# The expert stage of a diffusion step: plain fp32 on four column blocks, 96 tokens in three groups, in place of three rounded products of 128

## The chip, the cores and the metric

One core of a Trainium2 chip. The metric is the device time of one execution in microseconds. Lower is better.

## What is computed

One denoising step of a two-layer backbone on 128 context and 128 latent tokens, width D = 1024, all in fp32. Layer 0 is latent attention with a dense SwiGLU; layer 1 is a gated linear recurrence with a mixture of experts. Only the latter's expert stage is changed: 8 experts, hidden width 3584, each token goes to its two best, and the weights w1, w3 and w2 of all experts together are 352 MB.

```python
def moe_swiglu(h, router, w1, w3, w2):
    probs = jax.nn.softmax((h @ router).astype(F32), axis=-1)
    top_p, top_i = lax.top_k(probs, TOP_K)
    top_p = top_p / jnp.sum(top_p, axis=-1, keepdims=True)
    combine = jnp.sum(jax.nn.one_hot(top_i, N_EXPERTS, dtype=F32) * top_p[..., None], axis=-2)
    out = jnp.zeros_like(h)
    for e in range(N_EXPERTS):
        out = out + combine[..., e:e + 1].astype(h.dtype) * swiglu(h, w1[e], w3[e], w2[e])
    return out
```

The layer's result is x + gate * out, then a final RMSNorm over all 256 tokens (G = 2 groups of P = 128).

## The kernel before, in words

It is written engine by engine: each engine has its own program, in order, and waits on semaphores. What comes before the expert stage (modulation, attention, dense layer, recurrence, router) streams its weights through a ring of seven 2 MB slots.

**Tokens.** The router's plan gives every expert the list of its tokens, up to 128 at a time. POOL gathers an expert's rows from HBM by an indirect DMA (`gather`, L680), one expert ahead; PE turns them (`turn_gathered`, L1219), ACT takes them as a rounded high part (`take_gathered`, L1669), DVE takes the rest as a low part (`tokens_low`, L2139). If some expert has more than 128 tokens, a guarded second round ("again") runs all experts once more; otherwise it is skipped.

**Weights.** They come in pieces of 1 MB (128 x 2048), 42 an expert, into six buffers (`RAW`). The hidden width is cut into seven blocks of 512 (`EFB`); a block has two pieces of w1, two of w3 and two of w2. SP issues the loads (`load_piece` L601, `expert_loads` L615): four once the recurrence is done (`ro_done` 8, L622), every other one when the piece six before it has been split. ACT rounds each piece to a high part (`round_piece`, L1644), DVE subtracts to make the low part (`split_piece`, L2129); six buffers of each part.

**Products.** PE (`expert`, L1238) holds 128 tokens stationary and streams 512 columns of weights. Each block of 128 x 512 takes three products of rounded operands (`products`, L727 by way of `mm`): high with high, high with low, low with high. `gate_up` (L1239) does so for w1 into one bank and w3 into another; ACT takes SiLU of the first (L1712 and L1680 are its lines in `expert`), DVE multiplies (`hidden`, L2224), PE turns the 512 hidden columns (`transposes`, L1249), ACT and DVE split them in high and low (`hidden_high`, L1684; `hidden_low`, L2229), and PE multiplies them with w2 one block later (`down`, L1256). The order is written out by hand: w1 of block b, the transposes of b-1 in its midst, w3 of b, then w2 of b-1.

**Results.** ACT copies the expert's 128 rows of output and stores them in HBM (`store_first`, L1721); each expert has 256 rows there (`SLOTS`). POOL clears the upper half of each, and one more tile, in nine transfers of 512 KB (L657 to L661), from a tile that DVE zeroes (`zeros_set`, L2024) in time for DVE's wait before the recurrence (`late_cleared`, L2099). In the last expert POOL picks each token's two rows (`pick`, L701) by tables that DVE makes (`slot_tables`, L2186), ACT weighs them (L1716), DVE adds them to x (`mix`, L2214). The last expert's rows do not go through HBM: its output is multiplied by the layer's gate rows (L2272), spread to the tokens by a product with one-hot rows, and added (L2278), in halves of 512 columns (`down_by_half`, L1303). The final norm and four stores end the kernel.

**Loops.** On each engine seven experts run in a loop (`Fori(0, NE - 1)`; on SP and ACT the first expert is written out ahead of it) and the last is written out.

Other plain fp32 products on PE that the prediction reads: the modulation projection (`ada_products`, L777: eight products of 512 columns onto tiles of 32 array columns, four side by side), the attention scores (L1096) and the latent-attention projections (256 columns over the whole array). The recurrence's weights are rounded on ACT at L1475. `residual` (L1801) adds the mixer's output.

Of the kernel before, what the change touches and what calls it, by code (L numbers as in the profile page):

```python
# [15 lines left out]
P = 128  # L16
D = 1024
# [25 lines left out]
EFB = 512  # L43
EB = E_FF // EFB
PIECE = 2048
NPC = 6 * EB
RAW = 6
PARTS = 6
AHEAD = 4
SLOTS = 2 * P  # L50
# [77 lines left out]
def hybrid_step(nc, a, out):  # L128

    with ExitStack() as ctx:  # L130
# [9 lines left out]
        y_slots = nc.dram_tensor("expert_rows", (NE * SLOTS, D), F32, kind="Internal").ap()  # L140
# [116 lines left out]
        parts_hi, lo = rounded_tensor("weights_high", RAW * PIECE, (PARTS, PIECE))  # L257
        parts_lo, lo = rounded_tensor("weights_low", lo, (PARTS, PIECE))
        heT_hi, lo = rounded_tensor("tokens_high", lo, (DC, P))
        heT_lo, lo = rounded_tensor("tokens_low", lo, (DC, P))  # L260
        he_at = lo - 2 * DC * P
        hidT_hi, lo = rounded_tensor("hidden_high", lo, (2, EFB))
        hidT_lo, lo = rounded_tensor("hidden_low", lo, (2, EFB))
        h_tok, o = cut(lo - RING * SLOT, (G, D))
        gathered, y_e = h_tok[:, 0, :], h_tok[:, 1, :]
        e_silu, o = cut(o, (EFB,))
        e_hid, o = cut(o, (EFB,))
# [15 lines left out]
        token_of, o = cut(o, (2 * NE + 1,))  # L283
# [8 lines left out]
        e0_onehot, _ = cut(he_at - RING * SLOT + 2 * DC * P, (G, P))  # L292
        picked, late_picked = (raw[:, at:at + G, :].rearrange("p g (r n) -> p g r n", r=2) for at in (0, AHEAD))
        y_rows = h_tok
        y_gated = h_tok.rearrange("p g (h n) -> p g h n", h=2)
        squared, _ = cut(he_at - RING * SLOT, (G, D))

        psum = ctx.enter_context(nc.psum_tensor("banks", [P, 8, 512], F32))
        bank = [psum[:, i, :] for i in range(8)]

# [87 lines left out]
        last_gated, last_spread = sem("last_rows_gated"), sem("last_rows_spread")  # L388
        late_chain = sem("late_dve_chain")
# [3 lines left out]
        piece_landed = [sem(f"piece_landed{i}") for i in range(RAW)]  # L393
        rounded, split = sem("piece_rounded"), sem("piece_split")
        used = sem("piece_used")
        esilu, ehid = sem("expert_silu"), sem("expert_hidden")
        ehT, ehT_hi, ehT_lo = sem("hidden_transposed"), sem("hidden_high_taken"), sem("hidden_low_taken")
        he_hi, he_lo = sem("tokens_high_taken"), sem("tokens_low_taken")
# [88 lines left out]
        assert NPC % RAW == 0 and NPC % PARTS == 0  # L487

        def first_piece(b):
            return 6 * b - 2 if b else 0  # L490

        def piece_of(p):

            if p < 4:
                return ("w1", "w1", "w3", "w3")[p], 0, p % 2
            b, j = divmod(p - 4, 6)
            return (("w1", "w1", "w3", "w3")[j], b + 1, j % 2) if j < 4 and b + 1 < EB else ("w2", b, j % 2)

# [86 lines left out]
        def _(sp):  # L585
# [15 lines left out]
            def load_piece(p, e):  # L601

                dst = raw[:, p % RAW, :]
                name, b, half = piece_of(p % NPC)
                if name == "w2":
                    rows = bass.ds(e * E_FF + EFB * b + EFB // 2 * half, EFB // 2)
                    src = a["moe_w2"][0].rearrange("e f n -> (e f) n")[rows, :].rearrange("(p k) n -> p k n", p=P)
                    dst = dst.rearrange("p (k n) -> p k n", k=2)
                else:
                    rows = slice(D // 2 * half, D // 2 * (half + 1))  # L610
                    dst = dst.rearrange("p (k n) -> p k n", k=DC // 2)
                    src = a["moe_" + name][0, bass.ds(e, 1), rows, EFB * b:EFB * (b + 1)].rearrange("e (k p) n -> p (e k) n", p=P)
# [19 lines left out]
            with sp.If(again > 0):  # L632
                sp.wait_ge(split, NPC * NE)
                sp.wait_ge(mixed, G)
                for p in range(AHEAD):
                    load_piece(p, 0)
                with sp.Fori(NE, 2 * NE - 1) as it:
                    expert_loads(it, it - NE, it - (NE - 1))
                expert_loads(2 * NE - 1, NE - 1, 0)
# [12 lines left out]
        def _(pool):  # L652
# [55 lines left out]
            pool.wait_ge(y_stored, 16 * (NE - 1))  # L708
            for g in range(G):
                pool.wait_ge(split, NPC * (NE - 1) + NPC - RAW + g + 1)  # L710
                pick(0, g, picked)
            again = pool.value_load(over[0:1, 0:1], min_val=0, max_val=1)
            with pool.If(again > 0):
                pool.wait_ge(late_table, 1)
                pool.wait_ge(last_spread, 4)
                for it in range(NE, 2 * NE + 1):
                    gather(it)
                pool.wait_ge(y_stored, 16 * (2 * NE - 1))
                for g in range(G):
                    pick(1, g, late_picked)  # L720
# [4 lines left out]
        def _(pe):  # L725
# [493 lines left out]
            def turn_gathered():  # L1219
                for c in range(DC):  # L1220
                    last = pe.transpose(bank[5 + c // 4][:, P * (c % 4):P * (c % 4) + P], gathered[:, P * c:P * c + P], ident)  # L1221
# [16 lines left out]
            def expert(it, last_one=False):  # L1238
                def gate_up(b, which, half):  # L1239

                    p = first_piece(b) + 2 * which + half
                    pe.wait_ge(split, count_at(it, NPC, p + 1))
                    for k in range(DC // 2):
                        c = DC // 2 * half + k
                        w = [t[:, p % PARTS, EFB * k:EFB * (k + 1)] for t in (parts_hi, parts_lo)]
                        last = products(bank[which], (heT_hi[:, c, :], heT_lo[:, c, :]), w, c == 0, c == DC - 1)
                    last.then_inc(used, 1)

                def transposes(b):  # L1249
                    pe.wait_ge(ehid, count_at(it, EB, b + 1))  # L1250
                    for m in range(4):
                        cols = e_hid.rearrange("p (h n k) -> p h k n", h=2, k=2)[:, m // 2, m % 2, :]
                        last = pe.transpose(bank[4][:, P * m:P * m + P], cols, ident)  # L1253
                    last.then_inc(ehT, 1)

                def down(b, part):  # L1256
                    p = first_piece(b + 1) + 4 + part if b + 1 < EB else NPC - 2 + part
                    pe.wait_ge(split, count_at(it, NPC, p + 1))
                    pe.wait_ge(ehT_lo, count_at(it, EB, b + 1))
                    for k in range(2):  # L1260
                        m = 2 * part + k
                        x = [t[:, b % 2, P * m:P * m + P] for t in (hidT_hi, hidT_lo)]
                        for rest in range(2):
                            for half in range(2):
                                at = D * k + 512 * half
                                w = [t[:, p % PARTS, at:at + 512] for t in (parts_hi, parts_lo)]
                                last = mm(bank[2 + half], x[rest], w[0], b == m == rest == 0, b == EB - 1 and m == 3 and rest == 1)
                                if rest == 0:
                                    mm(bank[2 + half], x[0], w[1], False, False)
                    last.then_inc(used, 1)  # L1270

                pe.wait_ge(he_lo, count_at(it, 2, 2))
                for b in range(EB):
                    if b:
                        pe.wait_ge(esilu, count_at(it, EB, b))
                    gate_up(b, 0, 0)
                    if b:
                        transposes(b - 1)
                    gate_up(b, 0, 1)
                    gate_up(b, 1, 0)  # L1280
                    gate_up(b, 1, 1)
                    if b == 1:
                        pe.wait_ge(y_taken, count_at(it, 2, 1))
                    if b:
                        down(b - 1, 0)
                        if b == EB - 1:
                            transposes(b)
                        down(b - 1, 1)
# [1044 lines left out]
```

## Time and profile before

| | us |
|---|---|
| median of 3 runs | 1612.33 |
| lowest and highest run | 1611.0, 1616.38 |
| the profiled execution, its span | 1608.6 |
| PE busy | 1564.5 |
| DVE busy | 1173.0 |
| ACT busy | 988.2 |

The profile is of one execution. Busy times are summed over an engine's instructions; PE's matmuls are pipelined and their ends modelled, so a row's duration includes a drain that the next one overlaps. PEld is the loading of stationary operands. In a row "128*32" is the tile of the array, "x16" the number of instructions, and a plain fp32 product shows as two matmul instructions.

### The profile page before, as it was taken

The page shows a single profiled execution, that of the slowest core. Times are in us where ns is not written, and L with a number is a line of the kernel's source. Part 1 is how long each engine was busy: PE and PEld are TensorE (multiplying, and loading weights), DVE is VectorE, ACT ScalarE, POOL GpSimd, SP SyncE. Part 2 cuts the span into 40 slices and gives each one's busy share as a digit, 9 for nine tenths or more (in the row PEclk, how much of TensorE's full clock was granted, in tenths as well). Part 3 has the DMA queues.
Part 4 walks back from the last instruction along what each step waited for, and adds up shares of the span by engine and source line. Part 5 has one row for each costly group of instructions (what it writes and reads, how often), then busy time and mean ns, then how long its engine had stood idle before and what let it go on. Part 6 is the DMA issues. An engine that isn't in the chain of part 4 may idle for free.

```text
span 1608.6 us, 23366 instructions
## 1 busy us (share of the span) xinstructions
PE 1564.5 (97%) x9115; PEld 1316.4 (82%) x9115; DVE 1173.0 (73%) x1092; ACT 988.2 (61%) x983; POOL 39.4 (2%) x39
## 2 busy tenths in 40 slices
PE   6999999999999989999999999999999999999997
PEld 4976899898789778788888888888888888888885
DVE  2465444445755856988988988988988988888987
ACT  2445333334754546867767767777777777777674
POOL 0000000000010000000000000000000000000001
PEclk9999999999999999999999999999999999999999
DMA  9498397767474044999999999999999999999993
GB/s 364 161 326 306 106 364 257 270 222 275 157 280 152 23 170 156 384 386 367 383 386 364 378 381 371 381 382 369 374 392 363 378 389 358 386 371 365 381 380 136
DMA packets 201348, 498.30 MB, mean 310 GB/s; under 512 B 8591, under 2 KB 12222, under 8 KB 186942
## 3 DMA queue, kind: packets, MB, share of 16 engines
q1 hardware_dynamic: 194030, 477.96, 80.3%
q0 software_dynamic: 3984, 14.17, 2.6%
q10 hardware_dynamic: 3264, 5.19, 0.9%
q8 instruction: 49, 0.80, 0.2%
q14 instruction: 21, 0.17, 0.0%
HBM read 485.60 MB, written 11.69 MB: 309 GB/s over the span
## 4 chain that ended last, share of the span: by engine, by line
PE 53%; DVE 5%; issue 4%; ACT 3%; DVEq 0%; ACTq 0%
PE banks L727 51%; DVE weights_low L2129 2%; ACT weights_high L1644 2%; PE banks L1253 2%; DVE hidden_low L2231 1%; DVE tokens_low L2142 1%; DVE arena L2227 0%; PE banks L1221 0%; ACT hT L1366 0%; DVE ring L2077 0%; ACT arena L1758 0%; DVE arena L2305 0%; DVE arena L2272 0%; ACT L1680 0%; ACT L1653 0%
## 5 line engine op out<-in xcount | busy, mean ns | idle before, releaser
L2129 DVE TENSOR_TENSOR weights_low<-pieces,weights_high 128x2048 fp32r<-128x2048 f32 x336 | 754.1, 2286 | 131.0 <-ACT weights_high L1644 131.0
L1644 ACT CAST weights_high<-pieces 128x2048 fp32r<-128x2048 f32 x336 | 624.9, 1915 | 31.0 <-PE banks L727 25.0
L727 PE MATMUL banks<-weights_high,tokens_high 128*128 128x512 f32 x896 | 354.4, 396 | 0.7 <-DVE tokens_low L2142 0.7
L727 PE MATMUL banks<-weights_high,tokens_low 128*128 128x512 f32 x896 | 349.9, 391 | 0.0
L727 PE MATMUL banks<-weights_low,tokens_high 128*128 128x512 f32 x896 | 348.6, 389 | 0.0
L727 PEld LDWEIGHTS banks<-weights_high,tokens_low 128*128 128x128 f32 x896 | 168.2, 188 | 36.0
L727 PEld LDWEIGHTS banks<-weights_high,tokens_high 128*128 128x128 f32 x896 | 168.8, 188 | 33.7 <-issue 0.8
L727 PEld LDWEIGHTS banks<-weights_low,tokens_high 128*128 128x128 f32 x896 | 168.5, 188 | 33.7
L727 PE MATMUL banks<-weights_high,hidden_high 128*128 128x512 f32 x448 | 175.9, 393 | 3.0 <-DVE hidden_low L2231 3.0
L727 PE MATMUL banks<-weights_low,hidden_high 128*128 128x512 f32 x448 | 174.5, 389 | 0.0
L1684 ACT CAST hidden_high<-banks 128x512 fp32r<-128x512 f32 x56 | 32.9, 587 | 190.7 <-PE banks L1253 190.7
L727 PE MATMUL banks<-weights_high,hidden_low 128*128 128x512 f32 x448 | 138.7, 389 | 0.0
L727 PEld LDWEIGHTS banks<-weights_high,hidden_high 128*128 128x128 f32 x448 | 84.2, 188 | 23.1 <-DVE weights_low L2129 5.0
L727 PE MATMUL banks<-input_high,dense_high 128*128 128x256 f32 x352 | 100.9, 287 | 0.1
L727 PE MATMUL banks<-input_low,dense_high 128*128 128x256 f32 x352 | 99.5, 283 | 0.0
L727 PE MATMUL banks<-input_high,dense_low 128*128 128x256 f32 x352 | 99.5, 283 | 0.0
L727 PEld LDWEIGHTS banks<-weights_high,hidden_low 128*128 128x128 f32 x448 | 84.1, 188 | 17.8
L727 PEld LDWEIGHTS banks<-weights_low,hidden_high 128*128 128x128 f32 x448 | 84.1, 188 | 17.0
L1952 DVE TENSOR_TENSOR dense_low<-ring,dense_high 128x1024 fp32r<-128x1024 f32 x66 | 79.6, 1223 | 17.5 <-ACT dense_high L1468 17.5
L1972 DVE TENSOR_TENSOR hT<-hT,banks 128x256 f32<-128x256 f32 x22 | 9.3, 421 | 93.2 <-ACT hT L1488 93.2
L1959 DVE TENSOR_TENSOR ring_rounded<-ring,ring_rounded 128x2048 fp32r<-128x2048 f32 x24 | 54.8, 2290 | 30.4 <-ACT ring_rounded L1475 30.4
L1488 ACT ACTIVATE hT<-banks 128x256 f32<-128x256 f32 x22 | 8.4, 384 | 110.3 <-PE banks L727 110.3
(278 smaller groups left out, 2178.0 us busy)
## 6 DMA issues: line engine op xcount, KB each, us to landing
pieces<-in_moe_w SPq DMA_DIRECT2D x336, 1024.0 KB, 7.5
ring<-in_w_ada SPq DMA_DIRECT2D x24, 2048.0 KB, 11.8
ring<-in_ffn_w SPq DMA_DIRECT2D x15, 2048.0 KB, 11.9
ring<-in_hg_w_f SPq DMA_DIRECT2D x4, 2048.0 KB, 18.5
expert_rows<-arena POOLq DMA_DIRECT2D x9, 512.0 KB, 7.3
ring<-in_mla_w_o SPq DMA_DIRECT2D x2, 2048.0 KB, 17.8
ring<-in_hg_w_i SPq DMA_DIRECT2D x2, 2048.0 KB, 7.7
ring<-in_hg_w_q SPq DMA_DIRECT2D x2, 2048.0 KB, 7.6
```

What stands on the lines that cost most here:

```text
L727: return pe.matmul(o_, lhsT=l, rhs=r, start=start, stop=stop, skip_group_check=True)
L1253: last = pe.transpose(bank[4][:, P * m:P * m + P], cols, ident)
L1488: act.activation(silu_g[:, f % 2, :], bank[f % 2][:, 0:T], ACT.Silu).then_inc(silu_done, 1)
L1644: act.copy(parts_hi[:, p % PARTS, :], raw[:, p % RAW, :]).then_inc(rounded, 1)
L1684: act.copy(hidT_hi[:, b % 2, :], bank[4]).then_inc(ehT_hi, 1)
L1952: dve.tensor_tensor(dense_part(dense_lo, f, w), dense_source(f, w), dense_part(dense_hi, f, w).bitcast(F32), ALU.subtract).then_inc(up_spl ...
L1959: dve.tensor_tensor(rest[:, mixer_piece(h), :], whole[:, mixer_piece(h), :], high[:, mixer_piece(h), :].bitcast(F32), ALU.subtract).then_i ...
L1972: dve.tensor_tensor(hid[:, f % 2, :], silu_g[:, f % 2, :], bank[f % 2][:, T:2 * T], ALU.mult).then_inc(hid_ready, 1)
L2129: dve.tensor_tensor(parts_lo[:, p % PARTS, :], raw[:, p % RAW, :], parts_hi[:, p % PARTS, :].bitcast(F32), ALU.subtract).then_inc(split, 1)
L2142: dve.tensor_tensor(heT_lo[:, v, :], bank[5 + half].rearrange("p (a b) -> p a b", a=4), heT_hi[:, v, :].bitcast(F32), ALU.subtract).then_i ...
L2231: dve.tensor_tensor(hidT_lo[:, b % 2, :], bank[4], hidT_hi[:, b % 2, :].bitcast(F32), ALU.subtract).then_inc(ehT_lo, 1)
```

## The change

The expert stage is written anew. Rounding and splitting go, on ACT and DVE, with the buffers of their results. The pieces stay 1 MB and 42 an expert, but there are 14 buffers instead of six; SP loads 14 pieces ahead, in four steps that wait for earlier stages, and then each piece when PE has used the one 14 before it. The hidden width is cut in one block of 512 and three of 1024 columns, the 512 first.

PE works in plain fp32. An expert has up to 96 tokens, as three groups of 32. A group is the stationary operand of four products that stand side by side on the array, 32 of its columns each, and stream a quarter of the block's columns each. So partition 32 j + t of a result holds token t of a group and column quarter j. PSUM is cut into four places of two banks (gate, up, y, turned rows).

SiLU, the product and the copies of turned rows take 384 or 768 columns at once. The output is stored in four transfers an expert. The last expert's gated rows are spread by small products on four 32-row tiles for each group of tokens. The slots in HBM are 96 rows per expert and round, with up to three rounds; 13 tiles are cleared instead of nine.

The core of the diff (of `expert` and the tail the new lines alone):

```diff
-EFB = 512
-EB = E_FF // EFB
+CAP = 96
+TG = CAP // 32
+SUPER = ((0, 512), (512, 1024), (1536, 1024), (2560, 1024))
+NSB = len(SUPER)
 PIECE = 2048
-NPC = 6 * EB
-RAW = 6
-PARTS = 6
-AHEAD = 4
-SLOTS = 2 * P
+NPC = 3 * D * E_FF // (P * PIECE)
+RAW = 14
+ROUNDS = -(-G * P // CAP)
+ZERO_FROM = (NE - 1) * CAP
+ZERO_TILES = -(-(ROUNDS * NE * CAP - ZERO_FROM) // P)
...
+        PIECE_ORDER = (("w1", 0), ("w3", 0), ("w1", 1), ("w3", 1), ("w2", 0), ("w1", 2), ("w3", 2), ("w2", 1),
+                       ("w1", 3), ("w3", 3), ("w2", 2), ("w2", 3))
+        pieces = [(kind, sb, i) for kind, sb in PIECE_ORDER for i in range(SUPER[sb][1] // 256)]
+        assert len(pieces) == NPC
+        first_piece = {at[:2]: p for p, at in reversed(list(enumerate(pieces)))}
+        def pieces_end(kind, sb):
+            return first_piece[kind, sb] + SUPER[sb][1] // 256
+        BLOCKS_LANDED = [16 * sum(blocks[m][1] is not None for m in range(i, N0, RING)) if i < RING else 0 for i in range(RAW)]
+        RAW_AT = (4, 5, 0, 1, 2, 3, 6, 7, 12, 13, 8, 9, 10, 11)
+        def piece_at(p):
+            return raw[:, RAW_AT[p % RAW], :]
...
             def expert_loads(it, e, e_next):
 
-                for p in range(AHEAD, NPC + AHEAD if e_next is not None else NPC):
-                    if p >= RAW or not isinstance(it, int) or it > 0:
-                        sp.wait_ge(split, count_at(it, NPC, p - RAW + 1))
+                for p in range(RAW, NPC + RAW if e_next is not None else NPC):
+                    sp.wait_ge(used, count_at(it, NPC, p - RAW + 1))
                     load_piece(p, e if p < NPC else e_next)
 
+            sp.wait_ge(g_ready, 4)
+            for p in range(2):
+                load_piece(p, 0)
             sp.wait_ge(ro_done, 8)
-            for p in range(AHEAD):
+            for p in range(2, 6):
+                load_piece(p, 0)
+            sp.wait_ge(wo_ready, 6)
+            for p in range(6, 10):
+                load_piece(p, 0)
+            sp.wait_ge(wo_ready, 8)
+            for p in range(10, RAW):
                 load_piece(p, 0)
             expert_loads(0, 0, 1)
...
-            for e in range(NE + 1):
-                late = SLOTS * e + P if e < NE else SLOTS * (NE - 1)
-                pool.dma_start(y_slots[late:late + P, :],
+            for tile in range(ZERO_TILES):
+                at = ZERO_FROM + P * tile
+                pool.dma_start(y_slots[at:at + P, :],
...
+                def landed_piece(p):
+                    pe.wait_ge(piece_landed[p % RAW], count_at(it, TURN_LANDINGS, BLOCKS_LANDED[p % RAW] + 16 * (p // RAW + 1)))
+                    return piece_at(p)
+                def gate_up(kind, s):
+                    width, n = SUPER[s][1], SUPER[s][1] // 4
+                    place, nk = gate_place if kind == "w1" else up_place, PIECE // SUPER[s][1]
+                    if s:
+                        pe.wait_ge(esilu if kind == "w1" else ehid, count_at(it, NSB, s))
+                    for i in range(width // 256):
+                        w = landed_piece(first_piece[kind, s] + i)
+                        for kk in range(nk):
+                            k = nk * i + kk
+                            for t in range(TG):
+                                for j in range(4):
+                                    last = mm(place[32 * j:32 * j + 32, n * t:n * t + n], heT[:, k, 32 * t:32 * t + 32],
+                                              w[:, width * kk + n * j:width * kk + n * j + n], k == 0 and n * t % 512 == 0, k == DC - 1)
+                        last.then_inc(used, 1)
+                def turn_hidden(s):
+                    nh = SUPER[s][1] // 512
+                    pe.wait_ge(ehid, count_at(it, NSB, s + 1))
+                    if s:
+                        pe.wait_ge(ehT_taken, count_at(it, NSB, s))
+                    for t in range(TG):
+                        cols = e_hid[:, P * nh * t:P * nh * (t + 1)].rearrange("p (c h) -> p h c", h=nh)
+                        for h in range(nh):
+                            at = P * (nh * t + h)
+                            last = pe.transpose(turn_place[:, at:at + P], cols[:, h, :], ident)
                     last.then_inc(ehT, 1)
 
+                def down(s, parts):
+                    nh = SUPER[s][1] // 512
+                    pe.wait_ge(ehT_taken, count_at(it, NSB, s + 1))
+                    for i in parts:
+                        w = landed_piece(first_piece["w2", s] + i)
+                        for kk in range(2):
+                            j, h = (i, kk) if nh == 2 else (2 * i + kk, 0)
+                            first = s == i == kk == 0
+                            for t in range(TG):
+                                at = P * (nh * t + h) + 32 * j
+                                for jj in range(4):
+                                    last = mm(y_place[32 * jj:32 * jj + 32, 256 * t:256 * t + 256], hidT[:, s % 2, at:at + 32],
+                                              w[:, D * kk + 256 * jj:D * kk + 256 * jj + 256], first and t % 2 == 0,
+                                              s == NSB - 1 and i == parts[-1] and kk == 1)
+                        last.then_inc(used, 1)
+                pe.wait_ge(he_ready, count_at(it, 2, 2))
+                gate_up("w1", 0)
+                gate_up("w3", 0)
+                gate_up("w1", 1)
+                turn_hidden(0)
+                gate_up("w3", 1)
+                pe.wait_ge(y_taken, count_at(it, 1, 1))
+                down(0, range(2))
+                gate_up("w1", 2)
+                turn_hidden(1)
+                gate_up("w3", 2)
+                down(1, range(4))
+                gate_up("w1", 3)
+                turn_hidden(2)
+                gate_up("w3", 3)
+                down(2, range(2))
+                turn_hidden(3)
+                pe.wait_ge(esilu, count_at(it, NSB, NSB))
                 if last_one:
+                    pe.wait_ge(last_onehot, 1)
+                    for m in range(G * TG):
+                        g, t = m // TG, m % TG
+                        last = pe.transpose(gate_place[:, P * m:P * m + P], last_wide[:, g, P * t:P * t + P], ident)
+                    last.then_inc(last_turned, 1)
                 else:
+                    pe.wait_ge(gathered_in, count_at(it, 16, 16))
+                    turn_gathered()
+                down(2, range(2, 4))
+                down(3, range(4))
...
-            for half in range(2):
-                for g in range(G):
-                    pe.wait_ge(last_gated, 2 * half + g + 1)
-                    mm(bank[(0, 1, 5, 6)[2 * half + g]], onehot[:, g, 1, :], y_gated[:, g, half, :], True, True).then_inc(last_spread, 1)
+            pe.wait_ge(spreadT_taken, 1)
+            for g in range(G):
+                pe.wait_ge(last_gated, g + 1)
+                for t in range(TG):
+                    for j in range(4):
+                        rows = slice(32 * j, 32 * j + 32)
+                        last = mm(bank[4 * g + j][:, 0:256], last_spreadT[rows, g, P * t:P * t + P],
+                                  y_gated[rows, g, 256 * t:256 * t + 256], t == 0, t == TG - 1)
+                last.then_inc(last_spread, 1)
...
+            def expert(it, stored, last_one=False):
+                for s in range(NSB):
+                    width = SUPER[s][1] // 4 * TG
+                    act.wait_ge(used, count_at(it, NPC, pieces_end("w1", s)))
+                    if s:
+                        act.wait_ge(ehid, count_at(it, NSB, s))
+                    act.activation(e_silu[:, 0:width], gate_place[:, 0:width], ACT.Silu).then_inc(esilu, 1)
+                    if last_one and s == 2:
                         for g in range(G):
                             weigh(g, picked, 32)
                 if last_one:
                     return
+                act.wait_ge(used, count_at(it, NPC, pieces_end("w3", NSB - 1)))
+                take_tokens(it + 2, 0, bank[0])
+                take_tokens(it + 2, 1, bank[1])
                 act.wait_ge(used, count_at(it, NPC, NPC))
+                if stored is not None:
+                    act.wait_ge(y_stored, stored)
+                act.copy(y_e, y_place[:, 0:TG * 256]).then_inc(y_taken, 1)
+                act.wait_ge(y_taken, count_at(it, 1, 2))
+                rows = y_slots[0:ROUNDS * NE * CAP, :].rearrange("(i t p) (j n) -> i j p t n", t=TG, p=32, j=4)
+                for j in range(4):
+                    act.dma_start(rows[bass.ds(it, 1), j].rearrange("i p t n -> p (i t) n"),
+                                  y_e[32 * j:32 * j + 32, :].rearrange("p (t n) -> p t n", t=TG)).then_inc(y_stored, 16)
...
-            dve.wait_ge(late_cleared, 16 * (NE + 1))
+            dve.wait_ge(late_cleared, 16 * ZERO_TILES)
...
+                def hidden(s):
+                    width = SUPER[s][1] // 4 * TG
+                    dve.wait_ge(esilu, count_at(it, NSB, s + 1))
+                    dve.wait_ge(used, count_at(it, NPC, pieces_end("w3", s)))
+                    if s:
+                        dve.wait_ge(ehT, count_at(it, NSB, s))
+                    dve.tensor_tensor(e_hid[:, 0:width], e_silu[:, 0:width], up_place[:, 0:width], ALU.mult).then_inc(ehid, 1)
+                for s in range(NSB):
+                    width = SUPER[s][1] // 4 * TG
+                    hidden(s)
+                    if last_one and s == 0:
                         slot_tables()
+                    dve.wait_ge(ehT, count_at(it, NSB, s + 1))
+                    dve.tensor_copy(hidT[:, s % 2, 0:width], turn_place[:, 0:width]).then_inc(ehT_taken, 1)
+                    if last_one and s == 2:
+                        for g in range(G):
+                            mix(g, picked, 0).then_inc(mixed, 1)
...
+            dve.wait_ge(last_turned, 1)
+            dve.tensor_copy(last_spreadT[:, :, :], gate_place[:, 0:G * TG * P].rearrange("p (g n) -> p g n", g=G)).then_inc(spreadT_taken, 1)
+            dve.wait_ge(y_stored, 64 * (NE - 1))
+            dve.wait_ge(used, NPC * NE)
+            for g in range(G):
+                dve.tensor_tensor(y_gated[:, g, :].rearrange("p (t n) -> p t n", t=TG),
+                                  y_place[:, 0:TG * 256].rearrange("p (t n) -> p t n", t=TG),
+                                  gate_cols[:, g, :].unsqueeze(1).broadcast_to([P, TG, 256]), ALU.mult).then_inc(last_gated, 1)
             for half in range(2):
                 for g in range(G):
+                    dve.wait_ge(last_spread, g + 1)
+                    v = x_tok[:, g, 512 * half:512 * half + 512].rearrange("p (a b) -> p a b", a=2)
+                    dve.tensor_tensor(v, v, psum[:, 4 * g + 2 * half:4 * g + 2 * half + 2, 0:256], ALU.add).then_inc(mixed, 1)
```

## Rows read from the trace of the kernel before

**Rows 1.** The page, parts 1 and 2: engines, and 40 slices of the span

```profile
PE 1564.5 (97%) x9115; PEld 1316.4 (82%) x9115; DVE 1173.0 (73%) x1092; ACT 988.2 (61%) x983; POOL 39.4 (2%) x39
...
PE   6999999999999989999999999999999999999997
...
PEclk9999999999999999999999999999999999999999
DMA  9498397767474044999999999999999999999993
```

**Rows 2.** Stretch: us; PE, PEld, DVE, ACT, POOL busy; clock, DMA share, GB/s

```profile
860.00:980.00 120.00, 119.58 (x543) 98.84 (x542) 102.68 (x58) 87.13 (x61) 2.97 (x1) 1.00 1.01 375
```

**Rows 3.** The chain of waits in order of time: start us, us, what

```profile
654.18 16.38 PE banks L727 x72
...
861.25 2.15 issue
...
1508.03 0.47 PE banks L1253 x4
1508.50 16.38 PE banks L727 x72
...
1590.99 5.74 PE banks L727 x24
```

**Rows 4.** The groups by line, whole span: busy us, mean ns, idle before

```profile
L2129 DVE TENSOR_TENSOR weights_low<-pieces,weights_high 128x2048 fp32r<-128x2048 f32 x336 | 754.1, 2286 | 131.0 <-ACT weights_high L1644 131.0
L1644 ACT CAST weights_high<-pieces 128x2048 fp32r<-128x2048 f32 x336 | 624.9, 1915 | 31.0 <-PE banks L727 25.0 <-ACT arena L1712 5.0 <-issue 1.0
```

**Rows 5.** The timeline of PE at the stage's start: start us, us, what

```profile
638.18 0.49 PE L727 MATMUL banks<-weights_high,tokens_high 128*128 128x512 f32 x1 [0.69 <-DVE tokens_low L2142]
```

**Rows 6.** Stretches with loads of other run lengths; columns as in the second group

```profile
20.00:40.00 20.00, 16.36 (x108) 11.74 (x105) 4.43 (x15) 2.45 (x8) 0.00 (x0) 1.00 1.05 391
40.00:48.00 8.00, 8.00 (x39) 6.83 (x38) 2.95 (x9) 5.20 (x9) 0.00 (x0) 1.00 1.03 402
...
1020.00:1040.00 20.00, 20.00 (x91) 16.62 (x90) 17.66 (x11) 15.29 (x11) 0.00 (x0) 1.00 1.03 399
```

**Rows 7.** The timeline of plain fp32 work on PE and its loads

```profile
18.22 1.93 PE L727 MATMUL banks<-ring,cond 128*32 128x512 f32 x16 [0.40 <-DMA ring<-in_w_ada]
...
18.68 0.13 PEld L727 LDWEIGHTS banks<-ring,cond 128*32 128x32 f32 x4 [0.30 <-issue]
...
20.07 0.94 PE L727 MATMUL banks<-cst 128*128 128x128 f32 x6
...
39.21 14.06 PE L727 MATMUL banks<-hT,ring 128*128 128x256 f32 x64
...
550.64 1.53 PE L727 MATMUL banks<-ring 128*32 128x128 f32 x64
```

**Rows 8.** DMA queues: the span; 860 to 1340; 525 to 585; an issue

```profile
q8 instruction: 49, 0.80, 0.2%
...
q1 hardware_dynamic: 67270, 176.31, 98.5%
q0 software_dynamic: 576, 2.10, 1.1%
q10 hardware_dynamic: 576, 2.10, 1.1%
...
q8 instruction: 7, 0.11, 0.8%
...
arena<-in_moe_router ACTq DMA_DIRECT2D x1, 32.0 KB, 2.5
```

**Rows 9.** The waits of ACT for the gate weights: us, times, longest

```profile
ACT ring_rounded L1475 <- DMA ring<-in_hg_w_g: 5.5, 2, 3.9
```

**Rows 10.** The timeline after the last product: start us, us, what

```profile
1596.76 1.29 DVE L2272 TENSOR_TENSOR arena<-banks,xT 128x512 f32<-128x512 f32 x2 [1.00 <-PE banks L727]
...
1600.19 0.69 DVE L2278 TENSOR_TENSOR hT<-hT,banks 128x512 f32<-128x512 f32 x1 [0.17 <-PE banks L727]
```

More of the change, by code:

```diff
@@ L632, in _ @@
             with sp.If(again > 0):
-                sp.wait_ge(split, NPC * NE)
-                sp.wait_ge(mixed, G)
-                for p in range(AHEAD):
+                sp.wait_ge(used, NPC * NE)
+                for p in range(RAW):
                     load_piece(p, 0)
-                with sp.Fori(NE, 2 * NE - 1) as it:
-                    expert_loads(it, it - NE, it - (NE - 1))
-                expert_loads(2 * NE - 1, NE - 1, 0)
+                for r in range(1, ROUNDS):
+                    with sp.Fori(r * NE, (r + 1) * NE - 1) as it:
+                        expert_loads(it, it - r * NE, it - (r * NE - 1))
+                    expert_loads((r + 1) * NE - 1, NE - 1, 0 if r + 1 < ROUNDS else None)
             sp.end_ifs()
@@ L1220, in turn_gathered @@
                 for c in range(DC):
-                    last = pe.transpose(bank[5 + c // 4][:, P * (c % 4):P * (c % 4) + P], gathered[:, P * c:P * c + P], ident)
+                    last = pe.transpose(gate_place[:, P * c:P * c + P], gathered[:, P * c:P * c + P], ident)
                     if c % 4 == 3:
@@ L1238, in expert @@
             def expert(it, last_one=False):
[L1239 to L1253, printed above, removed]
-                    last.then_inc(ehT, 1)
[L1256 to L1263, printed above, removed]
-                            for half in range(2):
[L1265 to L1288, printed above, removed]
-                    if b == 3 and not last_one:
-                        pe.wait_ge(gathered_in, count_at(it, 16, 16))
-                        turn_gathered()
-                    if b == 3 and last_one:
-                        pe.wait_ge(last_onehot, 1)
-                        for g in range(G):
-                            last = pe.transpose(bank[5][:, P * g:P * g + P], onehot[:, g, 0, :], ident)
-                        last.then_inc(last_turned, 1)
@@ L2184, in _ @@
             last.then_inc(token_ready, 1)
-            dve.tensor_scalar(over[0:1, 0:1], small[0:1, 0, 6:7], P + 0.5, None, ALU.is_gt).then_inc(plan_ready, 1)
+            dve.tensor_scalar(over[0:1, 0:1], small[0:1, 0, 6:7], CAP + 0.5, None, ALU.is_gt).then_inc(plan_ready, 1)
             def slot_tables():
@@ L2203, in slot_tables @@
                 then(last)
-                dve.tensor_tensor(onehot[:, :, 0, :], onehot[:, :, 0, :], onehot[:, :, 1, :], ALU.add).then_inc(last_onehot, 1)
+                for g in range(G):
+                    wide = last_wide[:, g, :].rearrange("p (t j n) -> p t j n", t=TG, j=4)
+                    both = (onehot[:, g, r, 0:CAP].rearrange("p (t n) -> p t n", t=TG).unsqueeze(2).broadcast_to([P, TG, 4, 32])
+                            for r in range(2))
+                    last = dve.tensor_tensor(wide, *both, ALU.add)
+                last.then_inc(last_onehot, 1)
+                for j in range(4):
+                    dve.tensor_copy(gate_cols[32 * j:32 * j + 32, :, :], gate_rows[32 * j:32 * j + 32, :, 256 * j:256 * j + 256])
             late_count = [0]
```

275 lines of the change are left out of this document (76 added, 199 removed).

## The prediction, made before the changed kernel was run

> **What bounds the kernel now.** I read first the page's slices [rows 1]: from the sixteenth of the 40 slices on, some 640 us in, PE is busy 9 tenths in nearly every one, the granted clock is full, and the DMA engines show 9 as well. That stretch is the expert stage, and two resources look full at once. The table by stretch settles how PE stands [rows 2]: 119.6 us busy of 120, at a clock of 1.00, which is the 2.4 GHz level. The chain of waits in order of time [rows 3] shows what fills it: runs of 72 products in 16.38 us (0.2275 us a product of 512 columns) with four transposes between them. Seven such runs, 504 products, are one expert's: 114.7 us. The "issue" pieces and the pieces of DVE lie on the side branch of rounding and splitting, 754.1 / 8 = 94 us of DVE and 624.9 / 8 = 78 us of ACT an expert [rows 4], below PE's 114.7. From the first product at 638.18 [rows 5] to the end of the last at 1596.73 (1590.99 plus 5.74 [rows 3]) are 958.5 us: 119.8 an expert, 5.1 of it transposes.
>
> Is the DMA a second bound? The same table gives 375 GB/s at a share of 1.01 [rows 2]. But where its queue is always full it moves more: 391 with runs of 2 KB, 402 with runs of 3 and 4 KB, 399 with 2 and 8 KB mixed [rows 6]. So it has about 6% to spare; PE sets the pace, with the DMA close behind.
>
> The sum is made against the profiled execution, whose span is 1608.6 us; the median of the runs shown, 1612.33, is 3.7 above it, and I add that at the end. About 0.3%, 5 us, is what a measurement of this kernel can tell from no change.
>
> **The products.** A 128x512 block of weights cost three rounded products of 0.2275 us. Now it costs three groups of 32 tokens, each in plain fp32: two records a product, and four products side by side on 32 columns of the array each. I call four records that run together a round. That they do run together is in the trace: a step of the modulation projection is eight products of 512 columns onto 32-column tiles, 16 records, and takes 1.93 us [rows 7]. Single fp32 records of 256 columns over the whole array take 14.06 / 64 = 0.22 us [rows 7], hence 0.43 at 512; sixteen in a row would be 6.9 us, and four rounds of 0.43 are 1.7. Per expert:
> - the three blocks of 1024 columns: 2 matrices x 8 chunks x 3 groups x 2 records = 96 rounds a block, 288, of 256 columns;
> - w2: 28 chunks x 3 x 2 = 168 rounds of 256 columns. With the 288, 456 x 0.217 (0.22 less the last record's drain) = 99.0 us;
> - the block of 512: 96 rounds of 128 columns. Nearest row: 64 records, eight rounds of 128 columns and eight of 64, in 1.53 us [rows 7]; that is 12 rounds' worth, at most 0.128 each, about 0.11 without the drain. 96 x 0.11 = 10.6 us (12.3 at the upper end).
> - transposes: 21 of hidden rows and 8 of tokens instead of 28 and 8. Four take 0.47 us in the chain [rows 3], 0.117 each: 29 x 0.117 = 3.4 us.
> - five changes from tiles to the whole array and back: the step above ends 20.07 - 18.22 = 1.85 us after its start, 0.13 over four rounds; I take 0.2 for both ways, 1.0 us.
>
> Sum 114.0 us against 119.8. The gain per expert is modest because four passes at a quarter of the columns give back what the third rounded product saved; it comes mostly from 0.217 for two passes of 256 columns against 0.2275 for one of 512.
>
> **The weights.** Rounding and splitting go, so PE waits for landings alone. Cover needed: 42 pieces must land in 114 us. An expert's traffic is 44.0 MB of weights, 0.5 of gathered rows, 0.4 of stores and 0.3 of code (below), 45.3 MB; at 402 GB/s that is 112.6 us, just under PE. Fourteen buffers instead of six, filled before the stage begins, are 36 us of lead, so a small deficit is paid from it.
>
> **The feed of PE.** An expert was 543 products and transposes with as many weight loads, about 1,090 records [rows 2]; it becomes 2,237 with as many loads, 4,470. The queue of instruction code carried 49 pages of some 16 KB in all [rows 8], and none in 860 to 1340 us, where only three queues appear [rows 8]: the old loop body stayed where PE reads it. Whether a body four times as long stays is shown nowhere. If it does not, each of the six turns of the loop waits for a page: nothing at the lower end, and at the upper one a page's own time (0.2% of 16 engines' span over 49 [rows 8], 1.05 us) and the shortest DMA row's 2.5 us [rows 8], 3.6 us in all. The rows here say nothing nearer, so I take the middle, 1.8 x 6 = 10.8 us, ends 0 and 21.6.
> The Trainium skill (Runtime: NRT & Kernel Launch, Instruction fetch mechanics) says that PE holds 128 KiB, 2048 instructions, and that a taken branch to a page it does not hold must fetch it first; by that the upper half of this span is right. The trace agrees that 1,090 stay; no run here shows the rest.
>
> **Start, end and the rest.** The first product waited for the split of the tokens (0.69 us idle [rows 5]); without it the stage starts at 637.5. The ACT and DVE work before it was covered by PE's output products and stays off the path. SP now issues two pieces at the gate products, four where the first four went until now and eight at the output products; the router's small load on ACT's queue is of 32 KB, and the broadcast gate rows, which they may delay, are read in the last expert only. POOL clears 13 blocks of 512 KB instead of 9, about 5 us more beside the gate weights, for which ACT waits 5.5 us in all [rows 9]. PE has the other projections to run first, so this costs nothing, and up to 5 us without that cover. Behind DVE's wait on the clears stands the recurrence, which comes after those weights. ACT issues four stores an expert instead of one, right before a SiLU that is due 48 x 0.11 = 5.3 us later: hidden. The tail after the last product was 1608.6 - 1596.73 = 11.9 us [rows 3]; its first 4.15, to 1600.88 (1600.19 plus 0.69 [rows 10]), are a gating half, products and adds. Now both gating products of 768 columns stand there (1.29 / 2 for 512 [rows 10], so 0.95 each, 1.9), then the second group's 24 records, six rounds, 1.5 with the drain, then three adds of 0.69, 2.1, and some 0.5 of hops: 6.0, so the tail is 13.7. If the row tiles of those products do not run together, 24 records x 0.217 instead of a quarter, twice, add 7.8.
>
> 637.5 + 8 x 114.0 + 10.8 + 13.7 = 1574.0; that is 34.6 under 1608.6, so **1577.7 us**.
>
> **Rivals.**
> - *Slower: PE starves for instructions.* An expert's 4,470 records are 18.7 pages (49 pages carried some 11,700 records, the total less six repeats of the loop). It decides above 119.8 / 18.7 = 6.4 us a page. The densest long stretch before the stage brought seven pages in 60 us [rows 8], 8.6 us each; at that pace an expert takes 161 us, and the whole 637.5 + 1288 + 13.7 + 3.7 = 1943. For it: twice the records per us over the whole stage. Against: that stretch waited for ACT and DVE, and 64 records with their loads went in 1.53 us [rows 7], 12 ns each against the 25 needed. Chance 0.10.
> - *Faster by less: the DMA binds.* If it keeps to 376 GB/s, the last piece lands at 637.5 + (8 x 45.3 - 14.7) / 0.376 = 1562; with a piece's products and the tail, 1582 in the end. For it: a share of 1.01 already. Against: [rows 6]. Chance 0.13.
> - *Slower: the weight loads are not hidden.* Each round would then add its four loads, 0.13 us [rows 7]; 552 rounds make 72 us an expert and 2153 us in all. Against: the step of 1.93 us contains 16 loads and has room for none. Chance 0.03.
> The Trainium skill (TensorE: Matmul & The Clock Gate, Part 3) says that loads overlap running products only when their row group differs, and here all share the full 128 rows: that rule gives this rival. The 1.93 us step does not agree with it.
> - *It does not do what it says.* Over 96 tokens for one expert would run 16 more experts. The reference's router sends 55 to 75 of this input's tokens to each, so I give it nothing.
>
> **The numbers.** The forecast has 0.69, with 0.05 for mishaps around it. Low: no wait at the loop's turns and a few us less elsewhere, 1558. High: the DMA rival, then the upper ends of turns (+11), tail (+8) and narrow rounds (+13): 1606. Faster by over 0.3%: 0.69 + 0.13 and a fifth of the mishaps, 0.83; within: the rest of them, 0.04; slower: the two rivals, 0.13.
>
> **What would show it.** Right: PE rounds of four records 0.216 apart at 256 columns; 114 us between experts; no DVE or ACT group of 128x2048; code pages in every expert; a gap at each turn of the loop. Wrong: PE idle before products with the releaser "DMA pieces" (the DMA rival), "issue" idle on PE all through an expert (the feed), rounds over 0.25 (the loads), or a tail over 16 us.

## The result, and the profile after

The changed kernel takes 1628.37 us (median of 4 runs, 1625.64 to 1629.48) against 1612.23 for the kernel before: ratio 1.0098, 95% interval 1.0081 to 1.0115. It is slower by 1%, where 1577.7 and faster was forecast. The profiled execution's span is 1623.8 us against 1608.6.

First the page's busy times and the queue of instruction code, then two stretches of one row each (the columns of [rows 2]): one expert, and the first 2 us after a turn of PE's loop.

```profile
PE 1538.8 (95%) x22735; PEld 1147.2 (71%) x22735; DVE 408.5 (25%) x697; ACT 331.6 (20%) x560; POOL 27.5 (2%) x43
...
q8 instruction: 189, 3.10, 0.8%
```

```profile
882.00:1005.00 123.00, 115.54 (x2237) 77.70 (x2237) 6.85 (x8) 4.80 (x7) 0.94 (x1) 0.99 0.96 368
...
882.00:884.00 2.00, 2.00 (x40) 1.92 (x44) 0.00 (x0) 0.00 (x0) 0.00 (x0) 0.50 0.89 335
```

Rounding and splitting are gone (DVE from 1173.0 to 408.5 us [rows 1]), and PE is the bound as before. But an expert takes 123 us, not 119.8, and in it PE is busy for 115.5 only. Pages of code went from 49 [rows 8] to 189. The waits and the chain show what PE stood still for; the chain's piece is the turn from the first expert to the second. A page is a stretch of PE's instruction code, some 16 KB, that is fetched by DMA; "issue" is time in which PE waits for nothing else that the profile shows.

```profile
PE banks L746 <- issue: 44.9, 17, 5.0
```

```profile
753.95 4.93 issue
758.88 4.14 PE banks L746 x91
763.01 0.39 issue
763.40 7.19 PE banks L746 x256
770.59 1.92 issue
772.51 11.65 PE banks L746 x227
```

No wait on a landing of weights is among PE's waits in the stage. What it does wait for shows as "issue", and the runs below show that it is its own instructions: 4.90 to 5.05 us at each of the six turns of its loop, 29.8 us in all, and 14.6 us more in pieces of up to 2.8, each inside a block of 512 columns. And in the 2 us behind a turn, at a granted clock of 0.50, the 1.2 GHz level, PE runs 40 records, where 256 in 7.19 us are 71 in 2: it had just stood still for 5 us. (The 256 ran at a granted clock of 1.00.)

The start, 638.66 for 637.5, and the tail came nearly as forecast. First the first product in the timeline, then the chain from the last one (line 746 is the matmul helper, 2242 the gating):

```profile
638.66 1.60 PE L746 MATMUL banks<-pieces,arena 128*32 128x128 f32 x49
```

```profile
1594.52 15.72 PE banks L746 x288
1610.24 0.03 issue
...
1610.33 0.97 DVE arena L2242
1611.43 2.91 PE banks L746 x48
```

The last product ends at 1610.24, and the tail is 13.6 us (forecast 13.7). The 49.8 us between the forecast span, 1574.0, and 1623.8 lie in the stage between, save 1.2 of the start: 971.6 us, against 912 + 10.8.

### The profile page after: what moved, and what is told of

It is laid out like the page before. It is cut to its first block, busy times and chain, and to the rows that moved or that the text cites. A ratio compares the mean times of both kernels' runs of the same rounds, so it can differ in the third digit from the quotient of the medians.

```text
span 1623.8 us, 48798 instructions
## 1 busy us (share of the span) xinstructions
PE 1538.8 (95%) x22735; PEld 1147.2 (71%) x22735; DVE 408.5 (25%) x697; ACT 331.6 (20%) x560; POOL 27.5 (2%) x43
## 4 chain that ended last, share of the span: by engine, by line
PE 62%; issue 3%; DVE 1%; ACT 1%; DMA 0%; DVEq 0%; ACTq 0%; POOLq 0%
PE banks L746 59%; PE banks L1289 2%; PE banks L1240 0%; DVE ring L2069 0%; ACT hT L1396 0%; DMA out<-arena 0%; PE banks L1139 0%; DMA arena<-in_state_hgrn 0%; DVE arena L2273 0%; PE banks L1103 0%; ACT arena L1750 0%; ACT L1673 0%; DVE arena L2083 0%; ACT arena L1594 0%; ACT ring L1615 0%
## 5 line engine op out<-in xcount | busy, mean ns | idle before, releaser
L746 PE MATMUL banks<-pieces,arena 128*32 128x256 f32 (+1 forms) x17664 | 896.6, 365 | 44.5 <-issue 44.4
L746 PEld LDWEIGHTS banks<-pieces,arena 128*32 128x32 f32 x17664 | 588.8, 112 | 341.0 <-issue 53.4
L746 PEld LDWEIGHTS banks<-input_high,dense_high 128*128 128x128 f32 x352 | 67.4, 191 | 8.9 <-issue 8.9
L1498 ACT CAST dense_high<-ring 128x1024 fp32r<-128x1024 f32 x66 | 68.6, 1047 | 8.4 <-PE banks L746 8.1
L746 PE MATMUL banks<-input_high,ring_rounded 128*128 128x256 f32 (+1 forms) x384 | 68.4, 279 | 0.3 <-DVE latent_query_low L1870 0.3
L746 PEld LDWEIGHTS banks<-input_high,dense_low 128*128 128x128 f32 x352 | 67.4, 192 | 0.0
L746 PEld LDWEIGHTS banks<-input_low,dense_high 128*128 128x128 f32 x352 | 67.4, 192 | 0.0
L746 PE MATMUL banks<-ring_rounded,input_high 128*128 128x512 f32 x192 | 61.0, 399 | 0.0
L746 PEld LDWEIGHTS banks<-input_high,ring_rounded 128*128 128x128 f32 (+1 forms) x384 | 57.3, 179 | 0.6 <-issue 0.5
L746 PE MATMUL banks<-dense_hidden_high,dense_high 128*128 128x256 f32 x176 | 50.6, 287 | 0.3 <-DVE dense_hidden_low L1968 0.3
```

Source lines behind the costliest of these rows:

```text
L746: return pe.matmul(o_, lhsT=l, rhs=r, start=start, stop=stop, skip_group_check=True)
L1498: act.copy(dense_part(dense_hi, f, w), dense_source(f, w)).then_inc(up_rounded if w < 2 else down_rounded, 1)
```

## The experiments

Theory A: PE's code is fetched again after a taken branch, and the narrow block reads code faster than pages come. Rival B: the gap is a handshake between experts. Rival C: what makes a page late is the weights' traffic.

**No loop on PE.** Its seven looped experts are written out; other engines keep their loops.

```diff
-            with pe.Fori(0, NE - 1) as it:
+            for it in range(NE - 1):
                 expert(it)
             expert(NE - 1, True)
```

> The changed kernel with PE's seven experts written out one after another, no loop on PE (the other engines keep theirs). In the changed kernel PE stands still 29.8 us in six turns of its loop, 4.9 to 5.05 us each, runs its first rounds after each at half clock (some 1.9 us lost, 11 us in six), and stands still another 14.7 us in the first blocks of 512 columns. Theory A (PE's code must be fetched again after a taken branch): the six gaps and the slow rounds after them go, 41 us; the last expert, reached without a branch, still lost 3.0 us in its narrow block, so eight times that may stand where 14.7 stands now, 9 us: 1587 to 1597 us. Rival B (the gap is a handshake between experts: tokens, output, landings): the six gaps stay, 1628 us.

Measured: 1596.31 us (1592.21 to 1598.45), 0.9899 of before (0.9873 to 0.9924), so 32 us under the change and faster than the kernel before. The chain at the same turn:

```profile
735.37 0.87 PE banks L1240 x8
736.25 19.82 PE banks L746 x439
756.07 1.16 issue
757.23 3.70 PE banks L746 x128
760.93 2.24 issue
763.16 13.49 PE banks L746 x297
```

PE goes from w2 of one expert (the first 288 of the 439 records) into the next one's block of 512 without a stop: the same handshakes are there, and they cost nothing. B falls. The stops inside the narrow block (the one of 512 columns) remain, and grow from 14.6 to some 23.7 us over the eight experts; the expectation had allowed for eight times 3.0. Between two such stops stand 128 products, as in the row of 3.70, with as many weight loads. These 256 records are about a page: the whole kernel's 22,735 matmul records and as many loads, over 189 pages, are 241 a page.

**The block of 512 last,** loop kept.

```diff
-SUPER = ((0, 512), (512, 1024), (1536, 1024), (2560, 1024))
+SUPER = ((0, 1024), (1024, 1024), (2048, 1024), (3072, 512))
...
-                down(0, range(2))
+                down(0, range(4))
...
-                down(3, range(4))
+                down(3, range(2))
```

> The changed kernel, loop kept, with the block of 512 columns last instead of first. Theory A: the six gaps of 5 us stay, since the branch stays. The stalls inside the narrow block (14.7 us) are a question of rate (a page of code in 3.6 us instead of 7): if the rate alone makes them, they move with the block and the time stays at 1625 to 1632; if they need the empty queue after a branch, they go, and the time is 1613 to 1618. Rival B (handshake): the gap at the turn stays too; this run does not tell A from B.

Measured: 1638.03 us (1636.45 to 1640.84), 1.0157 of before (1.0129 to 1.0185), above both expectations. The chain from the second expert's last blocks into the third:

```profile
855.26 0.90 issue
856.16 3.69 PE banks L746 x127
859.85 2.49 issue
862.35 8.73 PE banks L746 x161
...
882.93 4.86 issue
887.79 33.75 PE banks L746 x576
...
922.46 31.22 PE banks L746 x576
```

The gap at the turn stays. The stops moved with the narrow block, so its rate makes them, not the branch in front of it. They add up to 23.8 us in seven experts, 9.2 more than with the block first, which is nearly all of the 9.7 us between the two kernels. The likely reason for the growth, which no run tests by itself: right behind a turn the landed pieces had filled the buffers while PE stood still, and in the changed kernel the DMA engines' share is down to 0.29 from 763 to 766 us, as this row has it:

```profile
763.00:766.00 3.00, 2.62 (x97) 2.60 (x100) 0.00 (x0) 0.00 (x0) 0.00 (x0) 1.00 0.29 44
```

The 576 wide records behind the turn took 33.75 us, with a granted clock of 0.50 in the first 5 us; without a turn in front such a run takes 31.22. So slow records cost 2.5 us here, and 1.4 to 2.8 behind the six turns.

**Both.**

> No loop on PE and the block of 512 columns last. Theory A: no gaps between experts, no half clock; if the narrow block starves by its rate alone, eight times up to 3 us stay, 1587 to 1597; if it starves only behind a gap, nothing stays, 1570 to 1578 us. Rival B: 1613 to 1628.

Measured: 1584.79 us (1582.33 to 1588.99), 0.9818 of before (0.979 to 0.9845): 2 us below the first expectation, 14 above the second. The chain through the second expert's end:

```profile
848.62 1.01 issue
849.64 1.82 PE banks L746 x57
...
854.26 1.45 issue
855.72 3.70 PE banks L746 x128
859.42 0.44 issue
859.86 5.39 PE banks L746 x96
...
866.60 41.58 PE banks L746 x768
```

The stops are still there, 18.9 us in the stage, all in the narrow block or, once, in the transposes between its two halves. In the last expert there are none: its weights had landed by then (the DMA engines' share is 0.10 from 1545 to 1551 us and 0.02 from 1551 to 1563, where its narrow block runs). That speaks for C.

**The traffic taken away.** From the fifteenth piece on a load brings 8 columns; what PE computes from then on uses old weights.

```diff
+                if part is not None:
+                    dst, src = dst[:, 0:1, 0:part], src[:, 0:1, 0:part]
                 sp.dma_start(dst, src).then_inc(piece_landed[p % RAW], 16)
...
-                    load_piece(p, e if p < NPC else e_next)
+                    load_piece(p, e if p < NPC else e_next, 8)
```

> The changed kernel, loop kept; from the fifteenth piece on each load of weights brings 8 columns instead of 2048, so PE multiplies with old weights and the DMA is nearly idle in the stage. If the gap at the turn is the wait of a page of code behind queued weights (rival C), it shrinks from 5.0 us to under 3 and the stalls in the narrow block vanish: 1590 to 1605 us. If the price is the branch's own (theory A without contention), the gaps stay at 4.5 to 5 us and the time at 1620 to 1630.

Measured: 1587.48 us in a single run, 2.5 below the expectation of C. The waits, a stretch of 120 us in the stage, and the chain at the first two turns and at the last expert (line 748 is the matmul helper here):

```profile
PE banks L748 <- issue: 16.7, 10, 2.7
```

```profile
860.00:980.00 120.00, 116.82 (x2292) 78.08 (x2284) 6.85 (x8) 4.79 (x7) 0.94 (x1) 1.00 0.07 12
```

```profile
752.75 2.22 issue
754.97 22.71 PE banks L748 x576
...
870.40 2.48 issue
872.88 2.80 PE banks L748 x91
...
1325.84 15.68 PE banks L748 x288
...
1443.06 36.52 PE banks L748 x864
```

With the DMA engines at 7% instead of 96, a turn costs 2.2 to 2.7 us instead of 5, and in the narrow block no stop is longer than 0.65. So both A and C hold: the branch back over this body waits for a page in any case, and the weights double the wait; the narrow block's stops are the weights' doing almost wholly. The last expert runs with no stop at all: its first 576 records take 36.52 - 15.68 = 20.84 us (the other 288 are w2 of the expert before, as in the row with 15.68), and the expert from 1458.74 to its last product 113.4 us.

**How long a body stays.** PE multiplies one of the three groups of tokens (the others are left out, in the products with w2 too), then two.

```diff
-                            for t in range(TG):
+                            for t in range(1):
```

> The changed kernel, loop kept; PE multiplies one of the three groups of tokens and leaves out the other two, so its loop body has some 1,550 matmul and load records instead of 4,474. Theory A: the body stays where PE reads it, no page of code comes in turns two to six, no gap of issue at the turns; PE then waits for weights, and the stage is bound by the DMA, 45.3 MB an expert at 390 to 402 GB/s, 113 to 116 us: 1560 to 1590 us in all. Rival B: a gap of 5 us at each turn that is not a wait for weights.

> The same with two of the three groups, some 3,000 records in the body. Theory A: if the limit lies between 1,550 and 3,000, pages come in every turn (about 12 an expert) and the gaps at the turns are there, at 3 to 5 us; if it lies above 3,000, none. The DMA binds here too: 1560 to 1600 us.

Measured: 1504.9 us with one group, 1518.0 with two. With one group the queue of code and PE's waits:

```profile
q8 instruction: 52, 0.85, 0.2%
```

```profile
PE banks L746 <- DMA pieces<-in_moe_w: 306.8, 290, 3.1
```

With two:

```profile
q8 instruction: 144, 2.36, 0.7%
```

```profile
PE banks L746 <- DMA pieces<-in_moe_w: 123.2, 185, 2.9
PE banks L746 <- issue: 57.8, 24, 6.2
```

A body of some 1,550 records stays: 52 pages, three more than in the kernel before, none of them between 860 and 1340 us, and no wait for instructions among PE's. The loop and its branch are there too, and a gap of 5 us could not hide in a wait for weights, of which the longest is 3.1: it is the fetch that a turn pays for, not the branch. A body of some 3,000 records comes anew in every turn: 56 pages from 860 to 1340 us. The Trainium skill (Runtime: NRT & Kernel Launch, Instruction fetch mechanics) puts PE's store at 2048 instructions, and says that a taken branch to a target outside the current window of two pages must fetch the page first. With the store both runs agree, 1,550 on one side and 3,000 on the other; with the window they do not, since 1,550 records are some six pages and the branch back over them fetched none. Both were faster than the low end that I expected, by 55 and 42 us. With one group two things make the 55: the weights came at 411 GB/s, where 402 was the most I had allowed (19 us over the stage), and the expectation left out the 14.7 MB that had landed ahead (36 us). With two groups, at 405 GB/s, the same two are 6 and 36 us.

```profile
860.00:980.00 120.00, 76.73 (x837) 32.39 (x829) 7.79 (x9) 4.79 (x7) 0.94 (x1) 0.71 1.03 411
```

**The narrow block spread out.** No loop on PE, the block of 512 last, its four pieces of w1 and w3 put between pieces of w2; the order of the loads follows.

```diff
+                down(1, range(2))
+                gate_up("w1", 3, (0,))
+                down(1, range(2, 4))
+                turn_hidden(2)
+                gate_up("w1", 3, (1,))
+                down(2, range(2))
+                gate_up("w3", 3, (0,))
+                down(2, (2,))
+                gate_up("w3", 3, (1,))
+                down(2, (3,))
+                turn_hidden(3)
```

> No loop on PE, the block of 512 columns last and its four pieces of w1 and w3 (2.7 us each) put one by one between pairs of pieces of w2, so that PE reads a page of code in about 5 us there instead of 3.6. In the run with the block of 512 last and no loop, PE stood still some 18 us in the stage, all but a little of it in that block. If the narrow block starves because it reads code faster than pages come through a busy DMA (theory A with rival C's contention), most of the 18 us goes: 1567 to 1573 us. If the stall comes with the change of width itself or with a wait between blocks, it stays or grows with the four changes more: 1583 to 1592.

Measured: 1576.04 us (1574.77 to 1580.55), 0.9771 of before (0.9753 to 0.9789). The chain at two of the spread blocks:

```profile
853.88 2.20 issue
856.09 9.89 PE banks L749 x190
...
974.54 0.57 issue
975.11 4.76 PE banks L749 x128
979.88 2.26 issue
982.14 0.91 PE banks L749 x9
```

The stops fall from 18.9 to 11.0 us, the time by 8.8, with the same products in another order. "Most of the 18 us" was expected to go, and less than half did; the time lies between the two expectations, 3 us above the first. So the rate inside the block counts, but a page in about 5 us seems still too fast for some pages; what the remaining stops need was not tested. This is the fastest version, 52 us under the change and 36 under the kernel before.

## Why the prediction was wrong

**The products** were right. Rounds of 256 columns are 15.68 / 72 = 0.218 us apart (forecast 0.217). The last expert, without stops, takes 113.4 us in the run without traffic (forecast 114.0), and a looped one would take 0.2 more for its eight transposes of tokens (0.87 us, where the last has six in 0.66), so the base of the stage is 7 x 113.6 + 113.4 = 908.6 us, not 912. Weight loads are hidden, since four of them fit into such a round: that rival is out. One reading beside the sum was off: 36 transposes of 0.117 are 4.2 us of an old expert, not 5.1; the rest is short waits.

**The feed of PE, at the turns.** This is the first step that failed. The prediction saw that a body four times as long might not stay, and priced a turn at 0 to 3.6 us, middle 1.8, from a page's own time and the shortest DMA row. The first is busy time and holds no waiting; the second, the router's load at 606.1 us, was taken while the DMA engines were nearly idle (a share of 0.04 from 606 to 607 us). The gap is 5.0 us, above even the upper end, and 19 us more in six turns than the 10.8 of the sum; without the weights it is 2.2 to 2.7, inside the range. And a part of the price was not in the sum at all: PE stands still, its granted clock falls to 0.50, and the first records behind the turn are slow. The turn at 753.95 has 4.14 + 7.19 + 11.65 = 22.98 us where 20.84 do without stops; the six lose 2.1 to 3.8 each.

**The feed of PE, inside an expert.** The second step that failed: the rival of starving was judged by a mean, 6.4 us a page over an expert, and given 0.10. In the changed kernel wide rounds, 128 products in 7.0 us, never waited. But the block of 512 columns has as many records a round in half the time, 128 products in 3.7 us, and there PE stopped for 14.6 us in all. So the rival came true in a sixth of the products (384 of 2,237 records), at a price far below the 1943 us that it was given: the sum should have had the two rates apart. What was held against the rival, 64 records with their loads in 1.53 us, is half a page in one burst, and tells nothing of how fast pages come. And the rise that it granted, "twice the records per us", fits no row: 4,470 in 114 us are 39 a us, 4.3 times the old expert's 9.1 and 1.4 times the 28 of the densest stretch (seven pages of 239 in 60 us). The Trainium skill (Runtime: NRT & Kernel Launch, Instruction fetch mechanics) calls the crossing of a page's end mostly hidden. With wide rounds the trace agrees; in narrow ones beside a busy DMA it does not, with stops of up to 2.8 us.

Together, in the stage: 908.6 + 29.8 (turns) + 14.6 (narrow block) leave 971.6 - 953.0 = 18.6 us for records that run slow. With no loop on PE the stage is 940.5 us (636.53 to 1577.03), and 908.6 + 23.7 leave 8.2: some 10 of the 18.6 go with the turns. How the rest splits between the clock and stops too short for the chain's pieces stays open.

**The DMA** did not bind, as forecast; that rival is out, and by more than I thought (411 GB/s in the run with one group).

**The range.** Its upper end, 1606, is the profiled sum of 1574.0 with the upper ends of turns, tail and narrow rounds; set on the DMA rival's 1582, as its sentence has it, they give 1614. Either way it held 21.6 us for the turns, where 29.8 were measured, and nothing for the clock and the stops of the narrow block.

## What to carry to other kernels

A loop on PE was free here while its body stayed where PE holds its code (1,550 records did, 3,000 did not); beyond that each turn waited for a page, twice as long beside the weights' traffic as without it, and the granted clock fell too. Writing the loop out gave 32 us, with nearly as many pages (180 for 189): code that runs straight on cost no stop in the wide blocks. Other engines were not tried. Price the instruction feed block by block, at the block's own rate of instructions, and put blocks of short instructions between blocks of long ones.

## What the hardware showed that I had not expected

- The wait for a page of code after a branch is 2.2 to 2.7 us with the DMA engines at 7%, and 4.9 to 5.05 with them at 96% (the changed kernel).
- The clock can be granted at half behind a stop as short as 2.2 us: 0.50 from 756 to 759 us in the run without traffic, after the stop that ended at 754.97. The length of the stop alone does not tell it: behind the next turn's 2.48 us, in the same run, the granted clock was 1.00 in each microsecond from 872 to 884, and the first 91 narrow records took 2.80 us, where the changed kernel took 4.14 at the half clock.

```profile
756.00:757.00 1.00, 1.00 (x28) 1.00 (x22) 0.00 (x0) 0.00 (x0) 0.00 (x0) 0.50 0.41 101
```
